# Token-major projections in pairs with 512 moving channels, and each convolution tap over all 512 tokens

## The chip, the cores and the metric

The kernel runs on one core of a Trainium2 chip. The metric is device time in microseconds (us). TensorE is called PE below, VectorE DVE, ScalarE ACT, GpSimd POOL, and the engine that issues the DMAs SP.

## What is computed

A decoder trunk of two layers on 512 tokens of 1024 channels, in float32:

```python
for l in range(L):
    h = rms_norm(x, attn_pre_g[l])
    u = jnp.einsum('bsd,de->bse', h, w_in[l])          # 1024 -> 10 blocks of 256
    u_conv, rq, rk, rv, rg, mq, mk, mv, u_pool = jnp.split(u, [...], axis=-1)
    y_a = conv_mixer(u_conv, ...)      # GLU, causal depthwise conv of 31 taps, LayerNorm, silu
    y_b = retention(rq, rk, rv, rg, ...)   # 4 heads, chunks of 128 tokens, group norm, gate
    y_c = moba_attention(mq, mk, mv)   # with 512 tokens in blocks of 256: causal attention
    y_d = pool_mixer(u_pool, ...)      # causal means over 2, 4, 8, 16 tokens
    y = jnp.einsum('bse,ed->bsd', jnp.concatenate([y_a, y_b, y_c, y_d], axis=-1), w_out[l])
    x = x + rms_norm(y, attn_post_g[l])
    h = rms_norm(x, ffn_pre_g[l])
    f = silu(h @ w_gate[l]) * (h @ w_up[l])            # 1024 -> 2816
    x = x + rms_norm(f @ w_down[l], ffn_post_g[l])
```

## The kernel before

**Numbers in two halves.** Each float32 matrix product is three float16 products (high x high, high x low, low x high; `split3`, L504). Weights come as slots of 128x2048 float32 (1 MB) in four parts. SP loads a part into one of four raw buffers (L443) once the buffer is free, that is once DVE has read it; ACT rounds it to a high half (`split_hi`, L790) and DVE takes the low half (`split_lo`, L1158). A split slot lies in a ring of eight; slot n may be written once PE has finished with slot n-8. The first three slots have raw homes of their own.

**PE's program** is a list of units (L89 to L97). W_in has ten slots of 256 channels. They go in three groups (MQ, MK, CONV_A, CONV_G; then MV, RQ, RK, RV; then POOL, RG), each group first for tokens 0 to 255 (s=0), then for 256 to 511 (s=1). A unit is 48 matmuls: two of something, eight k-tiles, three products. Slots in TOKEN_MAJOR hold 128 tokens still and move the slot's 256 channels (shown as ps<-ring,hT); the others hold 128 channels still and move 256 tokens (ps<-hT,ring). After the ten slots come W_out (OUT units, 512 wide, ps<-ring,U), gate and up, and down.

**Small work between.** Between any two triples of matmuls (a tick, `TICK0`, L109) PE may run small products: transposes, attention (moba) and retention products. The table AT (L120) says at which tick each stands. PE takes its instructions strictly in this order, so a small product whose input is late holds everything behind it. `moba_stage` 0 to 5 is attention for s=0, 6 to 11 for s=1; bank 5 of PSUM is shared by moba_Y, conv_T, conv_Y, ret_O and ret_Y, one after the other (`take`, L497).

**DVE and ACT** run lists written by hand (L1533, L1000). The convolution (`conv`, L1270) works on channels by tokens: for s=0 and for s=1 each, 31 taps x 2 channel blocks = 62 operations of 128x256 (two L1284, the rest L1287), each multiplying shifted input by a per-partition weight and adding to `cacc`. It can begin for s=0 once glu(0) has written its input, and s=1 once glu(1) has. Its 62 operations are strewn between others: splits, `m_max` (L1469, the row maxima of attention), rotations (L1334 to L1339), norms, `pool_windows` (L1438 to L1456). `conv_T` on PE transposes the finished `cacc`, `conv_norm` (L1300) takes its statistics.

## Time and profile before

| what | value |
|---|---|
| three runs | 1099.81, 1101.53 and 2939.43 us, median 1101.53 |
| the profiled execution: its own time | 1100.66 us |
| its span in the trace | 1098.9 us, 16669 instructions |
| PE matmul busy | 98% of the span, 6662 matmuls |
| DVE busy | 57%, 1419 instructions |
| ACT busy | 37%, 810 instructions |
| W_in stage of layer 0, first unit to first OUT unit | 14.17 to 164.77 us |
| W_in stage of layer 1 (its first transposes ahead of the first unit included) | 555.57 to 701.97 us |

The page adds up each engine's busy time over the whole span. What a change in the W_in stage is worth is read from the timeline of that stage: which engine's row says that it sat idle, and on whom. The mean duration of one matmul is longer than the distance from one to the next, because they overlap; the distance is a row's length divided by its count, after the last one's tail (0.16 us at 256 columns, 0.27 us at 512) is taken off. For DVE a lone operation's duration is about 0.08 us longer than the distance between two back to back.

### The profile page before, as it was taken

Reading aid. Unit: us, or ns where it says so; the run is one execution under the profiler, and the core shown is the slowest. Engines: PE = TensorE matmul, PEld = TensorE weight load, DVE = VectorE, ACT = ScalarE, POOL = GpSimd, SP = SyncE. Lnnn points to the kernel's source line nnn. Section 1 sums busy time; section 2 is a strip of 40 time slices with the busy share of each in tenths; the row PEclk is TensorE's granted clock in tenths of the full one; section 3 lists DMA queues with packets and bytes.
Section 4 is the critical chain, followed back from the end, with each engine's and each line's share of the span. In section 5 each row is a group of like instructions: output and inputs, shape, how many; then the busy total and the mean of one; then the engine's idle time right before and its main releaser. Section 6 shows DMA issues by size and latency. Waiting matters only on the chain.

```text
span 1098.9 us, 16669 instructions
## 1 busy us (share of the span) xinstructions
PE 1081.2 (98%) x6662; PEld 656.5 (60%) x6662; DVE 621.1 (57%) x1419; ACT 410.0 (37%) x810; POOL 5.2 (0%) x18
## 2 busy tenths in 40 slices
PE   8999999999999999999999999999999999999997
PEld 5887894695444444444488888748744444444443
DVE  6998998973432433322579889898633433422014
ACT  5636355553332332221244464456532322331000
POOL 1000000000000000000000000000000000000000
PEclk9999999999999999999999999999999999999999
DMA  8513212254324323323023150134623323232001
GB/s 310 172 56 102 92 40 97 96 166 142 115 77 153 109 83 115 114 79 115 1 79 115 40 151 5 43 111 154 183 86 115 116 96 115 91 101 77 1 20 58
DMA packets 58173, 109.64 MB, mean 100 GB/s; under 512 B 7025, under 2 KB 7281, under 8 KB 57969
## 3 DMA queue, kind: packets, MB, share of 16 engines
q1 hardware_dynamic: 58096, 108.58, 30.8%
q8 instruction: 53, 0.87, 0.3%
q14 instruction: 24, 0.19, 0.1%
HBM read 106.46 MB, written 2.10 MB: 99 GB/s over the span
## 4 chain that ended last, share of the span: by engine, by line
PE 91%; DMA 3%; DVE 3%; ACT 1%; SPq 1%; issue 1%; ACTq 0%; DVEq 0%
PE ps L508 84%; DMA raw<-weights_dram 3%; PE ps L512 3%; PE ps L716 1%; PE ps L700 1%; DVE ring L1158 1%; DMA xs<-x_dram 1%; DVE E L1287 1%; ACT ring L786 0%; PE ps L635 0%; SPq L453 0%; ACT gbc L786 0%; PE ps L677 0%; PE ps L638 0%; PE ps L620 0%
## 5 line engine op out<-in xcount | busy, mean ns | idle before, releaser
L508 PE MATMUL ps<-hT,ring 128*128 128x512 f16 (+1 forms) x3264 | 547.4, 329 | 0.0
L508 PEld LDWEIGHTS ps<-hT,ring 128*128 128x128 f16 x3264 | 319.1, 98 | 221.4
L508 PE MATMUL ps<-ring,U 128*128 128x512 f16 x1440 | 313.4, 379 | 0.0
L1158 DVE SCALAR_TENSOR_TENSOR ring<-raw,ring 128x512 f16<-128x512 f32 x368 | 231.2, 685 | 89.4 <-ACT ring L786 88.7
L786 ACT ACTIVATE ring<-raw 128x512 f16<-128x512 f32 x368 | 208.1, 621 | 126.6 <-PE ps L508 80.4
L508 PEld LDWEIGHTS ps<-ring,U 128*128 128x128 f16 x1440 | 140.8, 98 | 167.2 <-issue 0.3
L1490 DVE SCALAR_TENSOR_TENSOR R<-ps,R 128x512 f32<-128x512 f32 (+1 forms) x52 | 31.7, 609 | 256.2 <-ACT R L961 255.9
L508 PE MATMUL ps<-ring,hT 128*128 128x256 f16 x1152 | 133.3, 273 | 1.4 <-DVE hT L1247 1.3
L961 ACT ACTIVATE R<-ps 128x512 f32<-128x512 f32 (+1 forms) x52 | 27.6, 530 | 276.1 <-PE ps L508 276.0
L508 PEld LDWEIGHTS ps<-ring,hT 128*128 128x128 f16 x1152 | 112.1, 98 | 16.1 <-issue 1.9
L1287 DVE SCALAR_TENSOR_TENSOR E<-E,par 128x256 f32<-128x256 f32 x240 | 102.1, 479 | 0.2
L1175 DVE TENSOR_SCALAR small<-small 128x1 f32<-128x1 f32 x31 | 4.7, 150 | 84.9 <-ACT sink L796 76.3
L796 ACT ACTIVATE sink<-ps 128x1024 bf16<-128x1024 f32 x15 | 15.2, 1017 | 90.6 <-PE ps L508 90.6
L1497 DVE TENSOR_TENSOR U<-R,U 128x512 f16<-128x512 f32 (+1 forms) x52 | 31.2, 600 | 0.0
L786 ACT ACTIVATE gbc<-ps 128x128 f32<-128x128 f32 (+3 forms) x32 | 13.9, 434 | 42.6 <-PE ps L716 34.0
L786 ACT ACTIVATE U<-R 128x512 f16<-128x512 f32 (+1 forms) x52 | 28.9, 556 | 2.1 <-DVE R L1490 2.1
L786 ACT ACTIVATE U<-ps 128x256 f32<-128x256 f32 (+2 forms) x48 | 22.0, 485 | 17.9 <-PE ps L508 8.8
L512 PE MATMUL ps<-cst,E 128*128 128x128 f32 x176 | 24.0, 274 | 3.2 <-DVE E L1239 2.8
L807 ACT ACTIVATE ps<-xs 128x1024 f32<-128x1024 f32 x16 | 16.3, 1022 | 26.6 <-DVE xs L1207 21.3
L935 ACT ACTIVATE gbc<-ps,small 128x128 f32<-128x128 f32 (+3 forms) x32 | 16.8, 526 | 23.0 <-DVE small L1469 22.6
L512 PEld LDWEIGHTS ps<-cst,E 128*128 128x128 f32 x176 | 20.1, 141 | 6.7 <-DVE E L1239 2.7
L786 ACT ACTIVATE hT<-ps 128x1024 f16<-128x1024 f32 x16 | 16.3, 1019 | 17.8 <-PE ps L512 17.8
(109 smaller groups left out, 498.9 us busy)
## 6 DMA issues: line engine op xcount, KB each, us to landing
raw<-weights_dram SPq DMA_DIRECT2D x368, 256.0 KB, 3.3
gbc<-gains_dram SPq DMA_DIRECT2D x8, 512.0 KB, 6.2
xs<-x_dram SPq DMA_DIRECT2D x4, 512.0 KB, 7.0
U<-weights_dram SPq DMA_DIRECT2D x8, 256.0 KB, 7.9
out_dram<-xs SPq DMA_DIRECT2D x8, 256.0 KB, 2.0
cst<-consts_dram SPq DMA_DIRECT2D x1, 1296.0 KB, 12.2
bd<-pool_w_dram SPq DMA_DIRECT2D x8, 16.0 KB, 9.8
par<-params_dram SPq DMA_DIRECT2D x1, 76.0 KB, 6.7
```

Of the source, the lines that this page charges most:

```text
L508: ins = mm(dst, st, mv_, start=first and i == 0, stop=last and i == 2, **kw)
L512: return nc.tensor.transpose(dst, src, ident)
L700: mm(bank[b][:, 0:P * (t + 1)], mqT[r, t % 2, h // 2, :], mkT[r, h // 2, 0:P * (t + 1)], start=False, stop=True, skip_group_check=True).th ...
L786: return A(dst, src, ACT.Copy, scale=scale)
L796: A(sink[:, :], pair(t), ACT.Square, scale=UNSCALE * DM ** -0.5, accum_out=ssq[:, t:t + 1]).then_inc(y_sq, 1)
L807: A(pair(t), xs[:, t, :], ACT.Square, scale=DM ** -0.5, accum_out=ssq[:, 4 + t:5 + t]).then_inc(x_sq, 1)
L935: A(pr[:, h % 2, 0:w], bank[(4, 6)[h % 2]][:, 0:w], ACT.Exp, bias=nms[:, c:c + 1], accum_out=sums[:, c:c + 1]).then_inc(mP, 1)
L961: A(sil[:, n % 2, 0:P * len(tiles)], gu_tiles(f, tiles)[0], ACT.Silu, scale=UNSCALE).then_inc(sil_done, 1)
L1158: V.scalar_tensor_tensor(out=ring[:, slot % RING, 1, raw_part(part)], in0=raw_home(n)[0], scalar=W_SCALE, in1=ring[:, slot % RING, 0, raw_ ...
L1287: ins = V.scalar_tensor_tensor(out=cacc[:, c, :], in0=src, scalar=w, in1=cacc[:, c, :], op0=ALU.mult, op1=ALU.add)
L1490: V.scalar_tensor_tensor(out=fbuf[:, n % 2, 0:w], in0=gu_tiles(f, tiles)[1], scalar=UNSCALE * A_SCALE, in1=sil[:, n % 2, 0:w], op0=ALU.mul ...
L1497: V.tensor_tensor(fT[:, 1, f, span(tiles)], fbuf[:, n % 2, 0:w], fT[:, 0, f, span(tiles)], ALU.subtract).then_inc(f_lo, 1)
```

## The change

1. The token-major slots become pairs: MQ with MK, MV with RV, RQ with RK. The weights of a pair are laid out so that its eight parts are the eight k-tiles, each with 512 channels (256 of either). A unit is now one tile of 128 tokens against 512 moving channels: 24 matmuls instead of 2 x 24 with 256. In the first unit of each pair PE waits for each part by itself (all eight of both slots within that unit). Pairs finish tile by tile, so ACT copies (`moba_in`, `v_in`) and DVE rotates (`ret_rotate`, `moba_rotate`) one tile of both members at a time: as many operations, of the same sizes.
2. The convolution's taps run over all 512 tokens: 62 operations of 128x512 in a layer in place of 124 of 128x256. They can begin only when glu(1) is done, and conv_T(0) can begin only when all are done.
3. `cn` moves into `cacc`; the scaling of queries by 1/8 moves from one ACT copy to another.
4. The tables AT and the lists of DVE and ACT are written anew around this; the groups are now MQ+MK, CONV_A, CONV_G; MV+RV, RQ+RK; POOL, RG. A token-major unit is 8 ticks of 512-column triples, the others 16 ticks of 256.

```diff
-MQ, MK, CONV_A, CONV_G, MV, RQ, RK, RV, POOL, RG = range(10)
+MQ, MK, CONV_A, CONV_G, MV, RV, RQ, RK, POOL, RG = range(10)
-TOKEN_MAJOR = (RQ, RK, RV, MQ, MK, MV)
+PAIRS = {MQ: MK, MV: RV, RQ: RK}
...
-    UNITS += [(c, HALVES[s]) for s in range(2) for c in group]
+    for tiles in HALVES:
+        for c in group:
+            if c in PAIRS:
+                UNITS += [(c, (t,)) for t in tiles]
+            elif c not in PAIRS.values():
+                UNITS.append((c, tiles))
...
-        ("moba_stage", 6): 184, ("conv_T", 0): 186, ("moba_stage", 7): 208, ("ret_T", 0): 211,
+        ("moba_stage", 6): 170, ("conv_T", 0): 172, ("moba_stage", 7): 183, ("ret_T", 0): 185,
...
+                if slot in PAIRS:
+                    if pre:
+                        pe.wait_ge(h_lo, xno(pre, l, t) + 1)
+                    take(i % 4, *pair_read(l, slot, t))
+                    for k in range(KT):
+                        if k:
+                            between(k)
+                        if FIRST_OF[slot] == i:
+                            pe.wait_ge(lo_split, PARTS * (l * SLOTS + slot) + k + 1)
+                        r, cols = (l * SLOTS + slot + k // PARTS) % RING, raw_part(k % PARTS)
+                        last = split3(bank[i % 4][:, :], [ring[:, r, 0, cols], ring[:, r, 1, cols]],
+                                      [hT[:, 0, k, tok(t)], hT[:, 1, k, tok(t)]], k == 0, k == KT - 1, False)
...
             def conv_T(l, s):
-                pe.wait_ge(conv_sb, hs(l, s))
+                pe.wait_ge(conv_sb, l + 1)
                 take(5, convN_sb, 2 * hs(l, s))
...
-            def conv(l, s, n):
+            def conv(l, n):
+                if l not in taps_done:
+                    taps_done[l] = 0
+                    dve.wait_ge(hb_sb, hs(l, 1))
...
-                    src = hbuf[:, c, HALF * s + k:HALF * s + k + HALF]
+                    src = hbuf[:, c, k:k + S]
...
+                moba_rotate(l, 3)
+                glu(l, 1)
+                split_lo(z + 9)
+                conv(l, 7)
                 m_max(l, 0, 0)
-                conv(l, 0, 1)
                 m_max(l, 0, 1)
...
-                conv_norm(l, 0, lambda: conv(l, 1, 1))
-                ret_rotate(l, 0, 1)
-                conv(l, 1, 1)
+                conv_norm(l, 0)
+                split_lo(z + 11)
                 m_max(l, 2, 2)
                 m_max(l, 2, 3)
-                conv(l, 1, 1)
-                split_lo(z + 10)
-                zero(l)
+                pool_windows(l, 0)
                 ret_mask(l, 0)
```

**The first unit.** On PE, at the first matmuls of layer 0's W_in stage (unit MQ, then MK), before:

```order
L508 MATMUL ps<-ring,hT 128x256 [waits lo_split,h_lo]
L508 MATMUL ps<-ring,hT 128x256 x5
L508 MATMUL ps<-ring,hT 128x256 [waits lo_split]
L508 MATMUL ps<-ring,hT 128x256 x5
L508 MATMUL ps<-ring,hT 128x256 [waits lo_split]
L508 MATMUL ps<-ring,hT 128x256 x5
L508 MATMUL ps<-ring,hT 128x256 [waits lo_split]
L508 MATMUL ps<-ring,hT 128x256 x5
L508 MATMUL ps<-ring,hT 128x256 [waits h_lo]
L508 MATMUL ps<-ring,hT 128x256 x23
```

The same engine after the change, from the fourth k-tile of the first tile on:

```order
L520 MATMUL ps<-ring,hT 128x512 [waits lo_split]
L520 MATMUL ps<-ring,hT 128x512 x2
L520 MATMUL ps<-ring,hT 128x512 [waits lo_split]
L520 MATMUL ps<-ring,hT 128x512 x2
L520 MATMUL ps<-ring,hT 128x512 [waits lo_split]
L520 MATMUL ps<-ring,hT 128x512 x2
L520 MATMUL ps<-ring,hT 128x512 [waits lo_split]
L520 MATMUL ps<-ring,hT 128x512 x2
L520 MATMUL ps<-ring,hT 128x512 [waits lo_split]
L520 MATMUL ps<-ring,hT 128x512 x2
L520 MATMUL ps<-ring,hT 128x512 [waits h_lo]
L520 MATMUL ps<-ring,hT 128x512 x23
```

Before, four parts (one slot) are waited for in the first tile, one per two k-tiles, and the second slot comes a tile later; now all eight parts are waited for in the first tile, one per k-tile.

**Where the taps begin.** On DVE in layer 0, before, from glu(0) (E<-U,ps) to the first taps (E<-E,par) and the split of slot 7 (ring<-raw):

```order
L1263 SCALAR_TENSOR_TENSOR E<-U,ps 128x2x256 [waits glu_th,unit_done]
L1284 TENSOR_SCALAR E<-E,par 128x256 [waits hT_ps,hb_sb]
L1284 TENSOR_SCALAR E<-E,par 128x256
L1287 SCALAR_TENSOR_TENSOR E<-E,par 128x256 [waits dve_tick] x8
L1158 SCALAR_TENSOR_TENSOR ring<-raw,ring 128x512 [waits hi_split] x4
L1287 SCALAR_TENSOR_TENSOR E<-E,par 128x256 [waits dve_tick] x18
```

After, from the end of the last moba rotation over glu(1) to the taps and the first row maxima:

```order
L1355 TENSOR_TENSOR U<-E 128x8x16 [waits dve_tick]
L1279 SCALAR_TENSOR_TENSOR E<-U,ps 128x2x256 [waits glu_th,unit_done]
L1174 SCALAR_TENSOR_TENSOR ring<-raw,ring 128x512 [waits hi_split] x4
L1300 TENSOR_SCALAR E<-E,par 128x512 [waits hT_ps,hb_sb]
L1300 TENSOR_SCALAR E<-E,par 128x512
L1303 SCALAR_TENSOR_TENSOR E<-E,par 128x512 [waits dve_tick] x5
L1477 TENSOR_REDUCE small<-ps 128x1 [waits mS_ps] x2
L1303 SCALAR_TENSOR_TENSOR E<-E,par 128x512 [waits dve_tick] x12
L1477 TENSOR_REDUCE small<-ps 128x1 [waits mS_ps] x2
L1303 SCALAR_TENSOR_TENSOR E<-E,par 128x512 [waits dve_tick] x9
```

The taps moved from behind glu(0) to behind glu(1) and the split of slot 9, and m_max(0,0) stands behind seven wide taps.

**Where the taps end.** On DVE in layer 0, before, from the row scaling of attention tile 1 over the split of slot 9 to the end of half 0's taps and the low half of moba's output (U<-ps,U):

```order
L1480 TENSOR_TENSOR E<-ps,small 128x256 [waits dve_tick]
L1158 SCALAR_TENSOR_TENSOR ring<-raw,ring 128x512 [waits hi_split] x4
L1287 SCALAR_TENSOR_TENSOR E<-E,par 128x256 [waits dve_tick] x2
L1254 SCALAR_TENSOR_TENSOR U<-ps,U 128x2x256 [waits moba_hi]
L1469 TENSOR_REDUCE small<-ps 128x1 [waits mP,mS_ps] x2
L1303 BN_STATS small<-ps 128x6 [waits convT_ps]
```

After, the same place:

```order
L1303 SCALAR_TENSOR_TENSOR E<-E,par 128x512 [waits dve_tick] x2
L1174 SCALAR_TENSOR_TENSOR ring<-raw,ring 128x512 [waits hi_split] x4
L1303 SCALAR_TENSOR_TENSOR E<-E,par 128x512 [waits dve_tick] x12
L1270 SCALAR_TENSOR_TENSOR U<-ps,U 128x2x256 [waits moba_hi]
L1477 TENSOR_REDUCE small<-ps 128x1 [waits mP,mS_ps] x2
L1319 BN_STATS small<-ps 128x6 [waits convT_ps]
```

The last two narrow taps of a half have become the last twelve wide taps, ahead of the low half of moba_Y(0) that frees bank 5, and of conv_norm.

**Who waits.** On PE in layer 0, before, from the S products of attention stage 6 over conv_T(0) (ps<-cst,E):

```order
L700 MATMUL ps<-U 128x384 x2
L508 MATMUL ps<-ring,hT 128x256 x6
L512 MATMUL ps<-cst,E 128x128 [waits moba_y,conv_sb]
L512 MATMUL ps<-cst,E 128x128 x3
L508 MATMUL ps<-ring,hT 128x256 x18
L508 MATMUL ps<-ring,hT 128x256 [waits mv_sb]
```

After, the same place:

```order
L717 MATMUL ps<-U 128x384 x2
L520 MATMUL ps<-hT,ring 128x256 x6
L524 MATMUL ps<-cst,E 128x128 [waits moba_y,conv_sb]
L524 MATMUL ps<-cst,E 128x128 x3
L520 MATMUL ps<-hT,ring 128x256 x12
L520 MATMUL ps<-hT,ring 128x256 [waits v_sb,lo_split]
```

Both times conv_T(0) stands six matmuls behind stage 6 and waits for the low half of moba_Y(0) and for conv_sb; before, conv_sb meant the 62 narrow taps of half 0 with 18 and more matmuls of RQ behind it, now it means all 62 wide taps, and the stream behind it is that of POOL (ps<-hT,ring).

## Rows read from the trace of the kernel before

**Rows 1.** The page: busy time of each engine; its row of the granted clock.

```profile
PE 1081.2 (98%) x6662; PEld 656.5 (60%) x6662; DVE 621.1 (57%) x1419; ACT 410.0 (37%) x810; POOL 5.2 (0%) x18
...
PEclk9999999999999999999999999999999999999999
```

**Rows 2.** Busy time in two stretches: start:end length, each engine's busy us (instructions), clock, DMA.

```profile
14.17:164.77 150.60, 146.92 (x1293) 127.32 (x1294) 136.33 (x346) 77.26 (x166) 2.57 (x8) 1.00 0.35 111
...
555.57:701.97 146.40, 145.12 (x1293) 127.59 (x1292) 128.28 (x334) 70.86 (x154) 0.00 (x0) 1.00 0.26 80
```

**Rows 3.** Timeline of PE: start, length (us), line, operation, count [idle before <-releaser].

```profile
14.17 10.93 PE L508 MATMUL ps<-ring,hT 128*128 128x256 f16 x96 [0.69 <-DVE hT L1247]
...
59.40 0.27 PE L697 MATMUL ps<-cst 128*128 128x128 bf16 x2 [0.34 <-ACT U L786]
...
61.34 2.13 PE L508 MATMUL ps<-ring,hT 128*128 128x256 f16 x18
...
118.50 9.01 PE L508 MATMUL ps<-ring,hT 128*128 128x256 f16 x81
...
164.77 4.70 PE L508 MATMUL ps<-ring,U 128*128 128x512 f16 x21
...
169.74 10.52 PE L508 MATMUL ps<-ring,U 128*128 128x512 f16 x48
...
555.57 1.04 PE L512 MATMUL ps<-cst,E 128*128 128x128 f32 x8
...
602.08 5.40 PE L508 MATMUL ps<-ring,hT 128*128 128x256 f16 x48
...
701.97 5.34 PE L508 MATMUL ps<-ring,U 128*128 128x512 f16 x24
```

**Rows 4.** Timeline of DVE at the start of layer 0.

```profile
13.99 1.89 DVE L1158 SCALAR_TENSOR_TENSOR ring<-raw,ring 128x512 f16<-128x512 f32 x3
15.79 1.22 DVE L1247 SCALAR_TENSOR_TENSOR hT<-ps,hT 128x1024 f16<-128x1024 f32 x1
16.92 4.90 DVE L1158 SCALAR_TENSOR_TENSOR ring<-U,ring 128x512 f16<-128x512 f32 x8
```

**Rows 5.** Timeline of ACT: the first halves of two slots' splits.

```profile
42.50 1.24 ACT L786 ACTIVATE ring<-raw 128x512 f16<-128x512 f32 x2 [0.58 <-DMA raw<-weights_dram]
...
47.15 1.36 ACT L786 ACTIVATE ring<-raw 128x512 f16<-128x512 f32 x2 [0.63 <-DMA raw<-weights_dram]
```

**Rows 6.** Timeline of DVE, layer 0: taps, rotation, windows, split, norms.

```profile
53.62 7.21 DVE L1287 SCALAR_TENSOR_TENSOR E<-E,par 128x256 f32<-128x256 f32 x18
...
89.93 1.02 DVE L1469 TENSOR_REDUCE small<-ps 128x1 f32<-128x384 f32 x2
...
111.35 1.29 DVE L1469 TENSOR_REDUCE small<-ps 128x1 f32<-128x512 f32 x2 [0.26 <-PE ps L700]
...
120.37 0.68 DVE L1334 TENSOR_TENSOR E<-ps,cst 128x512 f32<-128x512 f32 x1
...
122.36 0.59 DVE L1390 TENSOR_TENSOR U<-U,ps 64x128 f32<-64x128 f32 x2
...
137.30 0.72 DVE L1438 TENSOR_TENSOR Z<-U 128x540 f32<-128x540 f32 x1
...
142.35 3.65 DVE L1287 SCALAR_TENSOR_TENSOR E<-E,par 128x256 f32<-128x256 f32 x9
...
154.11 2.49 DVE L1158 SCALAR_TENSOR_TENSOR ring<-raw,ring 128x512 f16<-128x512 f32 x4
...
163.33 0.76 DVE L1303 BATCH_NORM_STATS2 small<-ps 128x6 f32<-128x256 f32 x2 [0.20 <-PE ps L512]
...
166.95 1.11 DVE L1400 BATCH_NORM_STATS2 small<-U 128x6 f32<-128x64 f32 x8
...
170.86 0.17 DVE L1412 SCALAR_TENSOR_TENSOR small<-small 128x8 f32<-128x8 f32 x1
```

**Rows 7.** Groups by shape: line, engine, op, shapes, count | busy us, mean ns.

```profile
L1220 DVE SCALAR_TENSOR_TENSOR ps<-ps,small,gbc 128x512 f32<-128x512 f32 x8 | 6.0, 755 | 0.1
```

More of the change, by code:

```diff
@@ L98 @@
 NU = len(UNITS)
-UNIT_AT = {(slot, t): i for i, (slot, tiles) in enumerate(UNITS) for t in tiles}
+UNIT_AT = {(c, t): i for i, (slot, tiles) in enumerate(UNITS) for c in {slot, PAIRS.get(slot, slot)} for t in tiles}
 FIRST_OF = {slot: min(UNIT_AT[slot, t] for t in TILES) for slot in range(SLOTS)}
@@ L127 @@
-        ("ret_S", 1): 225, ("ret_O", 1): 229, ("moba_stage", 9): 258, ("ret_T", 2): 277,
-        ("moba_stage", 10): 280, ("ret_S", 2): 280, ("moba_stage", 11): 285, ("moba_Y", 1): 293,
-        ("ret_Y", 0): 299, ("ret_T", 3): 302, ("pool_Y", 0): 304, ("ret_O", 2): 304, ("ret_S", 3): 307,
-        ("ret_O", 3): 310, ("conv_T", 1): 315, ("conv_Y", 1): 327, ("ret_Y", 1): 343, ("pool_Y", 1): 350,
-        ("fpre_T", 0): 372, ("fpre_T", 1): 374, ("fpre_T", 2): 415, ("fpre_T", 3): 438, ("pre_T", 0): 955,
@@ new lines @@
+        ("moba_stage", 1): 114, ("moba_T", 2): 122, ("moba_stage", 2): 126, ("moba_stage", 3): 131,
+        ("moba_stage", 4): 142, ("moba_stage", 5): 148, ("moba_T", 3): 160, ("moba_Y", 0): 165,
+        ("moba_stage", 6): 170, ("conv_T", 0): 172, ("moba_stage", 7): 183, ("ret_T", 0): 185,
+        ("conv_Y", 0): 187, ("ret_S", 0): 190, ("ret_O", 0): 192, ("ret_T", 1): 192, ("moba_stage", 8): 192,
+        ("ret_S", 1): 196, ("ret_O", 1): 199, ("moba_stage", 9): 202, ("ret_T", 2): 206,
+        ("moba_stage", 10): 206, ("moba_stage", 11): 206, ("pool_Y", 0): 206, ("moba_Y", 1): 208,
@@ L145 @@
     },
 ]
+E_COLS = 7 * 2 * HALF + 2 * (CW - 1 + S) + 4
 PAR = {}
@@ L394, in unit_bank, with tile_bank, of_tile @@
             return UNIT_AT[(slot, 2 * s)] % 4
+        def tile_bank(slot, t):
+            return bank[UNIT_AT[(slot, t)] % 4][:, :]
+        def of_tile(buf, t):
+            return buf[:, 2 * G * t:2 * G * (t + 1)]
         def gu_tiles(f, tiles):
@@ L528, in unit @@
                 between(0)
-                by_parts = l == 0 and i == 0
-                if FIRST_OF[slot] == i and not by_parts:
+                if FIRST_OF[slot] == i and slot not in PAIRS:
                     pe.wait_ge(lo_split, PARTS * (l * SLOTS + slot + 1))
@@ L544, in unit @@
                                 between(KT * c + k)
[L545 to L552 removed]
+                            cols, rows = slice(P * c, P * (c + 1)), half(s)
                             last = split3(b256(b)[:, c, :], [w[0][:, k, cols], w[1][:, k, cols]],
[L554 to L555 removed]
+                                          [hT[:, 0, k, rows], hT[:, 1, k, rows]], k == 0, k == KT - 1, True)
                 elif wide:
@@ L663, in conv_T @@
                     for c in range(2):
-                        last = transpose(b256(5)[:, t, P * c:P * (c + 1)], cacc[:, c, tok(t)])
+                        last = transpose(b256(5)[:, t, P * c:P * (c + 1)], cacc[:, c, tok(2 * s + t)])
                 last.then_inc(convT_ps, 1)
@@ L1726 @@
         weights[:, slot] = by_col[:, :, :, blk].transpose(0, 2, 1, 3).reshape(L, P, SLOT)
+    for slot, other in PAIRS.items():
+        both = by_col[:, :, :, [BLOCK_OF[slot], BLOCK_OF[other]]].reshape(L, 2, KT // 2, P, 2 * G)
+        weights[:, slot:slot + 2] = both.transpose(0, 1, 3, 2, 4).reshape(L, 2, P, SLOT)
     out_k = [k + c for k in (4, 0, 2, 6) for c in range(2)]
```

347 lines of the change are left out of this document (153 added, 194 removed).

## The prediction, made before the changed kernel was run

> **What bounds the kernel now.** I read the page first: PE is busy for 98% of the span at the full granted clock, 2.4 GHz, DVE for 57% [rows 1]. So nothing is won by relieving DVE or ACT unless PE waits for them, and PE idles 17.7 us in all (1098.9 less 1081.2), part of it at the start and the end, which the change leaves alone. The change lies in the W_in stages, so I cut the busy times by these: in layer 0 PE is busy 146.9 of 150.6 us, DVE 136.3; in layer 1 145.1 of 146.4 and 128.3 [rows 2]. There both engines are nearly full, and PE's own waits, which the timeline marks (an example is the 0.34 us ahead of the first attention product), come to only 3.7 and 1.3 us [rows 2, 3]. The third view is the timeline of PE: where the units begin and how far apart matmuls start. The fourth is that of DVE: what its blocks cost, since the change makes PE wait for all of the convolution at once.
>
> **PE's stream.** 96 matmuls of 256 columns in 10.93 us look slow, but there the first weights are still arriving. Away from it 81 take 9.01 us: less the tail, 0.1093 us each. 48 of 512 columns take 10.52, less the tail 0.2135 each [rows 3]. Two narrow ones cost 0.2186, one wide one 0.2135: 0.0051 us saved on each of 576 pairs, **2.9 us**, 1.45 a layer. All the columns are still moved; halving the count of matmuls saves next to nothing. What such a small gain rests on is the distance between starts, not the mean duration.
>
> Of this the Trainium skill, TensorE: Matmul & The Clock Gate, section "Back-to-back issue gap", says that in a sustained stream 512 columns take about 131 ns per matmul. By it the pairs would save 576 x (0.2186 - 0.131), 50 us. The 48 wide matmuls of these rows started 0.2135 us apart, so I follow the rows and leave this as a rival.
>
> **The first unit.** Before, tile 0 needs four parts; slot 1 comes a tile later. Now tile 0 needs eight. DVE's three parts from 13.99 are ready at 14.7, 15.3 and 15.9; then stands h_lo of tile 1 (1.22 us), and the parts of slot 1 come from 16.92 on at 0.60 us each, the first at 17.60 [rows 4]. PE starts at 14.17 and spends 3 x 0.2135 = 0.64 us per k-tile, so it wants part 4 at 16.75 and gets it 0.85 to 0.9 us later. After that DVE delivers every 0.60, faster than PE eats. Cost **0.9 us**, once: in layer 1 these slots were split long before. Nothing gives it back, since PE is the bound.
>
> **The taps.** 18 narrow ones take 7.21 us, less 0.08 for the last 0.396 each [rows 6]. A wide one with a per-partition scalar isn't in the trace as a tap. The nearest row is L1220, the same operation with such a scalar on 128x512: 0.755 us alone [rows 7], less 0.08 of overlap 0.67. Lower bound: the split, 512 wide without such a scalar, 2.49 us for four, 0.60 each [rows 6]; upper bound 0.755. I take 0.67: 62 cost 41.5 us. The 124 narrow ones at 0.396 cost 49 back to back, and about 3 more where they are strewn singly. DVE gains some 10 us a layer. That alone is worth nothing to PE, beyond the 3.7 and 1.3 us of waits.
>
> The Trainium skill, VectorE: DVE Perf Modes, section on the TRN2 errata, gives 58 cycles plus the elements at 0.96 GHz for an operation out of SBUF, 0.33 and 0.59 us. By it DVE would gain only 124 x 0.33 - 62 x 0.59 = 4 us a layer, but with wide taps of 0.59 the chain below would end 5 us earlier and PE's floor would hold. The narrow taps' 0.396 us shows that a tap costs more than that formula has, so I keep the rows' price.
>
> **When the taps can begin.** Here is the price of the change. They wait for glu(1), which was behind the second unit of CONV_G. In layer 0 PE reached the MV unit at 61.34 [rows 3]. Subtract attention stage 0, which now comes later (0.6), the waits up to there (about 0.9) and the stream (0.5), add the first unit's 0.9: 60.2. Then come on ACT the tanh (0.6) and four high halves of slot 9 (2.2), on DVE the last low half (0.7): taps from **63.7**. Until then DVE has only splits. Each slot takes about 4.65 us round the four raw buffers (42.50 to 47.15 [rows 5]), so slots 5 to 9 from 41 on end at about 64 too; this doesn't come first, but it would not let the taps begin earlier. In layer 1 MV began at 602.08 [rows 3]; less stages 0 and 1 and one transpose (2.0) and 0.5: 599.6, taps from 603.1.
>
> **The chain of DVE.** From there to the end of the taps: 41.5, eight short row maxima 2.2, two rotations of 2.0 (120.37 to 122.36), two scalings 1.1, the split of slot 10, 2.4, and the low half of moba_Y, 0.6 [rows 6]. Sum 51.8: 115.5 in layer 0. PE wants conv_T(0) 64 ticks of 0.641, 12 of 0.328 and about 10 us of small products after 60.2: 115.1. So this wait is 0.4 us at my tap price, and 5 us more at the upper one (60 x 0.085). Behind conv_T(0) stand attention stage 7, ret_T(0) and everything up to W_out.
>
> Then DVE still has, up to ret_mask(3), four splits 9.6; four pairs of row maxima (1.02 and 1.29 a pair, two of each, less the overlap) 4.4; conv_norm 3.6 (163.33 to 166.95); pool_windows 5.0 (137.30 to 142.35); ret_norm 4.1 (166.95 to 170.86 and its length); two rotations 4.0; masks, states, products, scalings and low halves about 9.6 [rows 6]. Sum 40.3. Without a wait that is 155.8. But now PE's small products stand close (stages 7 to 11, all ret products in 40 ticks of 0.328 us), so DVE waits for PE and PE for DVE in turn, where formerly single taps filled such holes. I count 5 us of such idle time, as between 2 and 9: a dozen hand-overs at 0.2 to 0.8 us, sized like the waits in [rows 3]. So ret_mask(3) at 160.8, ret_O(3) and conv_T(1) 1.6: W_out begins at 162.4, against 164.77: **-2.4 us**. Layer 1: 603.1 + 51.8 + 40.3 + 5 + 1.6 = 701.8, against 701.97: **-0.2 us**. PE's own floor would be 159.1 and 700.5 (busy 145.1 less 1.45, and 0.9 in layer 0), so the DVE chain ends last in both layers, by 1 to 3 us.
>
> **W_out.** DVE has about 26 us of work from its begin to the low half of ret_y(1), and PE needs that 40 ticks of 0.641 and 2 us later, 28. I take no wait; it would be 1 or 2 us a layer if the chain comes late. Copies and rotations are as many and as wide as before and lie beside PE. The feed-forward stages are untouched: 0.
>
> **Sum.** 1098.9 - 2.4 - 0.2 = 1096.3 us of span. The profiled execution took 1100.66, 1.8 more than its span, and the median of the runs is 0.9 above that: 1096.3 + 1.8 + 0.9 = **1099 us**. In this sum stream and first unit are already inside the layers' ends.
>
> **Rivals.**
> - *All waits go (0.15).* If the hand-overs cost no more than 2 us, PE's floor holds: -5.7 in layer 0, -1.5 in layer 1, 1094. For it: DVE's total falls to about 126 and 118 us in stages of 146. Against it: the work is pressed into the last 95 us.
> - *The convolution becomes the bound (0.27, of it 0.02 beyond 2%).* Wide taps near 0.75 and hand-overs of 9 us: 5 + 4 more in each layer, and 2 in W_out, about +15 in the worst case, +6 (1107) in its middle. It decides from a tap of 0.70 on, where conv_T(0) waits over 2 us and DVE ends later than before.
> - *The matmuls get cheap (0.01).* 50 us less, 1050. Against it stand the distances in [rows 3].
> - *The first unit waits much longer (0.02).* If slot 1's parts were late by a whole landing (some 3 to 5 us), 1103. Against it: both slots come early in [rows 4].
>
> **How the numbers follow.** My forecast, DVE's and PE's ends within a few us of each other, has 0.55: 1096 to 1103. The likeliest is its sum, 1099. Range: down to the floor, less a little, 1092; up into the slower rival, 1110. Over 2% is 22 us, about what a measurement of this kernel can tell from no change: a gain of that size exceeds all of PE's idle time, so 0.015; a loss of that size needs 10 us in each layer, 0.025; within 2%, 0.96.
>
> **What would show it.** 576 matmuls ps<-ring,hT of 512 columns at 0.2135 us; a wait of 0.9 us in the first unit; 120 taps of 128x512, mean 0.75 us, 0.67 apart; DVE's busy time down by 18 to 21 us to about 601; conv_T(0) waiting 0 to 3 us for DVE; new short waits of PE between conv_T(0) and W_out, 3 to 6 us a layer; W_out beginning near 162 and near 699. Wrong would be: taps starting well after 64, a W_in stage longer than 150 us, or a wait in W_out.

## The result: 6.5 us slower, where 2 us less were forecast

The changed kernel took 1107.66 us (median of 4 runs, 1106.72 to 1109.29) against 1101.12 for the kernel before in the same comparison, a ratio of 1.0062 with a 95% interval from 1.0050 to 1.0074. (One execution of the kernel before took 2939.43 us; it is in that median of four, but the ratio goes by the fast runs alone.) By the 2% bound that is no change, and inside the range. But the forecast had the sign wrong. The profiled execution took 1107.27 us with a span of 1105.4, against 1098.9 before.

The page of the changed kernel, to be read beside [rows 1]: busy times and the two groups that are new.

```profile
span 1105.4 us, 15389 instructions
...
PE 1080.5 (98%) x6086; PEld 600.5 (54%) x6086; DVE 607.5 (55%) x1295; ACT 408.2 (37%) x810; POOL 5.1 (0%) x18
...
L520 PE MATMUL ps<-ring,hT 128*128 128x512 f16 x576 | 128.3, 379 | 1.4 <-DVE ring L1174 0.7
...
L1303 DVE SCALAR_TENSOR_TENSOR E<-E,par 128x512 f32<-128x512 f32 x120 | 81.1, 744 | 0.0
```

Every engine has less to do, and the span is longer. The W_in stages answer to [rows 2]: start:end, length, then busy us (instructions) of PE, PEld, DVE, ACT and POOL, granted clock, DMA share, GB/s.

```profile
13.69:165.07 151.38, 145.78 (x1004) 99.56 (x1005) 130.77 (x282) 75.89 (x167) 2.57 (x8) 1.00 0.35 113
555.85:707.27 151.42, 145.52 (x1005) 99.68 (x1004) 125.39 (x276) 71.67 (x158) 0.00 (x0) 1.00 0.25 79
```

Layer 0's stage is 0.8 us longer than before, layer 1's 5.0. From W_out of layer 0 (165.07) to layer 1's W_in (555.85) it is 390.8 us in both kernels. From W_out of layer 1 to the end it is 1.2 us more. The first unit begins 0.5 us earlier; I count that to the start-up and not to the change, since in the traces of the variants below, all with the same start, it begins anywhere from 13.34 to 14.24 us. Sum: 0.8 + 5.0 + 1.2 - 0.5 = 6.5.

The place shows when the last 50 us ahead of W_out are set beside each other, layer 0 and layer 1 (same columns). Before:

```profile
114.77:164.77 50.00, 49.76 (x445) 44.39 (x445) 46.56 (x134) 20.58 (x43) 0.00 (x0) 1.00 0.20 64
651.97:701.97 50.00, 49.83 (x449) 44.48 (x446) 46.52 (x136) 20.64 (x43) 0.00 (x0) 1.00 0.20 59
```

And after, from conv_T(0) on (115.07 and 657.07):

```profile
115.07:165.07 50.00, 46.02 (x388) 38.66 (x387) 41.74 (x116) 32.49 (x74) 0.00 (x0) 1.00 0.28 91
657.07:707.27 50.20, 45.93 (x388) 38.61 (x387) 41.76 (x116) 33.88 (x76) 0.00 (x0) 1.00 0.28 90
```

PE idled 0.2 us there and now idles 4.0 and 4.3; DVE idled 3.4 and now idles 8.3 and 8.4. Both engines wait for each other more, with less work on either. The timeline of PE names the two waits (start, length, operation, count, [idle before <- releaser]); layer 0, then layer 1:

```profile
115.07 0.60 PE L524 MATMUL ps<-cst,E 128*128 128x128 f32 x4
115.51 3.77 PE L520 MATMUL ps<-hT,ring 128*128 128x256 f16 x33
120.61 0.52 PE L524 MATMUL ps<-cst,gbc 128*128 128x128 f32 x3 [1.34 <-ACT E L865]
...
128.91 1.10 PE L652 MATMUL ps<-U,R 128*128 128x64 f32 x8 [1.27 <-DVE R L1387]
...
662.61 0.52 PE L524 MATMUL ps<-cst,gbc 128*128 128x128 f32 x3 [1.67 <-ACT E L865]
...
670.90 1.10 PE L652 MATMUL ps<-U,R 128*128 128x64 f32 x8 [1.76 <-DVE R L1387]
```

The first row is conv_T(0). 33 narrow matmuls (11 ticks, 3.8 us; in layer 1 it is 10 ticks) later stage 7 wants bank 5, which conv_T(0) filled and which comes free only after conv_norm(0) on DVE and conv_scale(0) on ACT (L865). Next ret_O(0) waits for ret_mask(0) (L1387). On DVE the rows between are, in this order (the last of each block):

```profile
115.71 0.76 DVE L1319 BATCH_NORM_STATS2 small<-ps 128x6 f32<-128x256 f32 x2 [0.18 <-PE ps L524]
...
119.25 0.16 DVE L1331 SCALAR_TENSOR_TENSOR small<-small 128x2 f32<-128x2 f32 x1
119.33 2.49 DVE L1174 SCALAR_TENSOR_TENSOR ring<-raw,ring 128x512 f16<-128x512 f32 x4
122.12 1.02 DVE L1477 TENSOR_REDUCE small<-ps 128x1 f32<-128x384 f32 x2 [0.30 <-PE ps L717]
123.06 0.71 DVE L1446 TENSOR_TENSOR Z<-U 128x540 f32<-128x540 f32 x1
...
127.64 0.42 DVE L1464 SCALAR_TENSOR_TENSOR Z<-E,U 64x256 f32<-64x256 f32 x1
128.10 0.76 DVE L1387 TENSOR_TENSOR R<-ps,cst 128x256 f32<-128x256 f32 x2
```

conv_norm(0) 3.7 us, a split 2.5, two maxima 1.0, pool_windows(0) 5.0, then the mask: 13 us of DVE, of which 12.6 busy, while PE has only 10.9 us of work between conv_T(0) and ret_O(0) (10.4 in layer 1). Before, conv_T(0) ran at 90.49 us and 66 narrow matmuls stood between it and the next product:

```profile
90.49 0.60 PE L512 MATMUL ps<-cst,E 128*128 128x128 f32 x4
90.93 7.37 PE L508 MATMUL ps<-ring,hT 128*128 128x256 f16 x66
98.14 0.49 PE L512 MATMUL ps<-cst,gbc 128*128 128x128 f32 x3
```

### The profile page after: what moved, and what is told of

Its sections match the earlier page's. It is cut to its first block, busy times and chain, and to the rows that moved or that the text cites. A ratio compares the mean times of both kernels' runs of the same rounds, so it can differ in the third digit from the quotient of the medians.

```text
span 1105.4 us, 15389 instructions
## 1 busy us (share of the span) xinstructions
PE 1080.5 (98%) x6086; PEld 600.5 (54%) x6086; DVE 607.5 (55%) x1295; ACT 408.2 (37%) x810; POOL 5.1 (0%) x18
## 4 chain that ended last, share of the span: by engine, by line
PE 93%; DVE 4%; DMA 1%; ACT 1%; issue 1%; SPq 0%; ACTq 0%; DVEq 0%
PE ps L520 85%; PE ps L524 3%; PE ps L733 1%; PE ps L717 1%; PE ps L652 1%; DMA xs<-x_dram 1%; DVE ring L1174 0%; DMA raw<-weights_dram 0%; DVE E L1303 0%; PE ps L637 0%; PE ps L694 0%; ACT E L865 0%; DVE Z L1464 0%; ACT gbc L803 0%; DVE small L1155 0%
## 5 line engine op out<-in xcount | busy, mean ns | idle before, releaser
L803 ACT ACTIVATE ring<-raw 128x512 f16<-128x512 f32 x368 | 207.1, 621 | 123.6 <-PE ps L520 78.7
L520 PE MATMUL ps<-ring,hT 128*128 128x512 f16 x576 | 128.3, 379 | 1.4 <-DVE ring L1174 0.7
L520 PEld LDWEIGHTS ps<-ring,hT 128*128 128x128 f16 x576 | 56.2, 98 | 65.2 <-DVE ring L1174 2.3
L1303 DVE SCALAR_TENSOR_TENSOR E<-E,par 128x512 f32<-128x512 f32 x120 | 81.1, 744 | 0.0
L803 ACT ACTIVATE U<-ps 128x256 f32<-128x256 f32 (+2 forms) x48 | 22.1, 488 | 51.2 <-PE ps L524 32.5
L803 ACT ACTIVATE U<-R 128x512 f16<-128x512 f32 (+1 forms) x52 | 28.9, 556 | 3.2 <-DVE R L1498 3.2
L803 ACT ACTIVATE hT<-ps 128x1024 f16<-128x1024 f32 x16 | 16.2, 1017 | 28.3 <-PE ps L524 28.3
L803 ACT ACTIVATE gbc<-ps 128x128 f32<-128x128 f32 (+3 forms) x32 | 13.9, 435 | 27.0 <-PE ps L733 15.4
```

The costliest lines, as they stand in the source:

```text
L520: ins = mm(dst, st, mv_, start=first and i == 0, stop=last and i == 2, **kw)
L803: return A(dst, src, ACT.Copy, scale=scale)
L1303: ins = V.scalar_tensor_tensor(out=cacc[:, c, :], in0=src, scalar=w, in1=cacc[:, c, :], op0=ALU.mult, op1=ALU.add)
```

## Experiments: what the loss hangs on

All ratios are against the kernel before, which ran beside each on the same chip; the changed kernel stands at 1.0062.

**Too much work ahead of conv_T(0)?** The forecast's slower rival was that the taps become the bound.

```diff
-                for i in range(taps_done[l], min(taps_done[l] + n, 2 * CW)):
+                for i in range(taps_done[l], min(taps_done[l] + n, 2 * CW - 20)):
```

> The changed kernel with the last 20 of the 62 wide taps of each layer left out (the convolution is then incomplete), 13.3 us less work for DVE ahead of conv_T(0). Theory VOLUME (too much work on DVE ahead of conv_T(0), or a tap price that makes the convolution the bound): the waits of PE behind conv_T(0) go and the time falls to 1.000 of before or under. Theory CHAIN or PLACE (latency behind conv_T(0)): DVE just waits longer for conv_T(0), stage 7 waits 1.3 and 1.7 us and ret_O(0) 1.3 and 1.8 us as they do now, time 1.005 to 1.006 of before.

1107.48 us, 1.0060 (1.0048 to 1.0072). DVE is busy 38.72 of the 52.25 us from the first tap to conv_T(0), 13 us less than in the changed kernel, and nothing changes: stage 7 waits 1.34 and 1.67, ret_O(0) 1.27 and 1.76, to the hundredth. At 0.66 us a tap, neither the volume ahead of conv_T(0) nor the price of a tap costs anything.

```profile
62.82:115.07 52.25, 51.38 (x289) 28.34 (x288) 38.72 (x70) 14.00 (x41) 0.00 (x0) 1.00 0.12 39
```

The other direction, each wide tap as two of 256 at its place:

```diff
-                        ins = V.scalar_tensor_tensor(out=cacc[:, c, :], in0=src, scalar=w,
+                        for s in range(2):
+                            ins = V.scalar_tensor_tensor(out=cacc[:, c, half(s)], in0=src[:, half(s)], scalar=w,
```

> The changed kernel with each wide tap as two of 256 tokens at the same place, still behind glu(1): 62 x (2 x 0.396 - 0.662) = 8.1 us more for DVE ahead of conv_T(0) in each layer. Price of the row: PE waits some 8 us more for conv_T(0) in each layer, so 16 us and, if TensorE's clock falls behind so long a wait, up to 4 us more in each layer: 1.020 to 1.029 of before. If DVE had room ahead of conv_T(0): under 1.012.

1123.68, 1.0197 (1.0179 to 1.0216), just under the 1.020 that the price of the row gave. PE waits at conv_T(0) itself, now 3.35 and 2.70 us, and further up for ACT's steps of attention (1.45 and 1.10 us in layer 0, 1.53, 1.28 and 1.10 in layer 1), and part of the work behind the waits runs at a lower clock (last section). So the wide taps had just made room; without them the joined convolution would have cost some 16 us more.

**Products merely too early?**

```diff
-        ("moba_stage", 6): 170, ("conv_T", 0): 172, ("moba_stage", 7): 183, ("ret_T", 0): 185,
-        ("conv_Y", 0): 187, ("ret_S", 0): 190,
+        ("moba_stage", 6): 170, ("conv_T", 0): 172, ("moba_stage", 7): 187, ("ret_T", 0): 188,
+        ("conv_Y", 0): 189, ("ret_S", 0): 190,
```

> The changed kernel with attention stage 7, ret_T(0) and conv_Y(0) moved to later ticks (187 to 189), in both layers, so that matmuls of W_in fill the 1.34 and 1.67 us that stage 7 waits. ret_O(0) stays at tick 192, since the unit at tick 192 needs the rotation behind it. Nothing is left out. Theory PLACE (the products merely stand too early): stage 7 waits for nothing, the waits of the layer fall by 1.3 and 1.7 us, time 1.006 - 0.0027, near 1.0035 of before. Theory CHAIN (DVE's work between conv_T(0) and ret_mask(0), some 13 us, is longer than PE's 11): the wait only moves, stage 7 is free of it, ret_O(0) waits 2.6 and 3.4 us instead of 1.27 and 1.76, and the time stays at 1.006 of before.

1108.91, 1.0075 (1.0063 to 1.0087). Stage 7's wait is gone, and ret_O(0) waits 2.07 us in both layers, ret_T(0) 0.64. The wait moved, as theory CHAIN has it: with ret_T(0)'s it is 2.7 us in each layer, for 2.9 and 3.4. The medians differ by 1.3 us and their intervals overlap; in the trace the groups behind the longer wait of layer 0 run at a lower clock, which costs 1.3 us (last section).

```profile
123.33 0.63 PE L524 MATMUL ps<-cst,R 128*128 128x128 f32 x4 [0.64 <-ACT gbc L951]
128.70 1.64 PE L652 MATMUL ps<-U,R 128*128 128x64 f32 x8 [2.07 <-DVE R L1387]
```

**Cutting the chain.** One Newton step instead of three in conv_norm(0), or pool_windows(0) reduced to one memset, or both.

```diff
-                n = tick(rsqrt(slice(8, 10), fill))
+                n = tick(rsqrt(slice(8, 10), fill, 3 if s else 1))
...
+                if s == 0:
+                    V.memset(pooled_w, 0.0).then_inc(pool_sb, 1)
+                    return
```

> The changed kernel with one instead of three Newton steps in conv_norm(0) in both layers (the convolution's scale of the first half is then less exact), 1.38 us less of DVE between conv_T(0) and stage 7. Theory CHAIN: all behind stage 7 comes 1.3 us earlier in each layer, stage 7 waits 0 and 0.3 us, ret_O(0) still 1.3 and 1.8 us, time 2.7 us lower, 1.0035 of before. If it is the products' distance behind (PLACE) or ACT that decides: the wait comes back within the layer, over 1.005.

1104.81, 1.0031 (1.0017 to 1.0044). Stage 7 waits 0 and 0.29, ret_O(0) 1.26 and 1.76 as before.

> The changed kernel with pool_windows(0) cut down to one memset in both layers (the pooling branch of the first half is left out), 4.7 us less of DVE ahead of ret_mask(0). Theory CHAIN: ret_O(0) waits under 0.5 us instead of 1.27 and 1.76, stage 7 as now, time 2 to 3.5 us lower, 1.003 to 1.0045 of before, with no more than that, since the rest of DVE's work waits for PE's products. Theory VOLUME behind conv_T(0): DVE's 4.7 us are worth 4.7 us in each layer, 0.998 of before.

1104.83, 1.0032 (1.0021 to 1.0043). Stage 7 waits 1.33 and 1.67 as ever, ret_O(0) nothing and 0.38. 4.7 us of DVE work left out were worth 1.5 us a layer: what the wait had.

> The changed kernel with both cuts at once, one Newton step instead of three in conv_norm(0) (less exact) and pool_windows(0) reduced to a memset (the pooling branch of the first half left out), in both layers. Alone each brought 2.9 us. Theory CHAIN (conv_norm(0) and pool_windows(0) stand one after the other in one chain from conv_T(0) to ret_mask(0)): both gains add, stage 7 and ret_O(0) wait under 0.7 us together per layer, 5.8 us under the changed kernel, 1.0005 of before, so that these two waits account for about the whole loss. If the two cuts relieve the same wait, or another wait takes over: 1.002 to 1.003.

1101.65, 1.0003 (0.9994 to 1.0012). Both gains add: 6.0 of the 6.5 us, and what is left is within the interval. So the two waits are as large as the loss. They are not each layer's own loss: in the traces layer 0's W_in stage is now 1.3 us shorter than before the change, while from one W_out to the next, layer 1's W_in stage included, it takes 539.4 us against 537.2 before and 542.2 in the changed kernel. Layer 1 keeps other waits (below).

**Moving instead of cutting.** The first try put the mask ahead of all of pool_windows(0):

```diff
-                pool_windows(l, 0)
                 ret_mask(l, 0)
+                pool_windows(l, 0)
```

> The changed kernel with ret_mask(0) ahead of pool_windows(0) on DVE, in both layers; nothing is left out. Theory CHAIN: ret_O(0) waits at most 0.8 us instead of 1.27 and 1.76; DVE stands idle some 3.5 us until ret_S(0) is there, and works this off in its idle stretches behind; time 1.0035 to 1.005 of before. Theory VOLUME (DVE is the bound from there to W_out): the idle 3.5 us come back as waits before W_out, 1.008 of before or more. Theory PLACE has no say on it beyond CHAIN's.

1118.00, 1.0154 (1.0141 to 1.0167). The time lies where theory VOLUME put it (1.008 or more), but neither theory had the mechanism. ret_O(0) indeed stopped waiting for the mask, but ret_state(0) (L1398) now stood behind pool_windows(0), and it frees bank 6 for stage 8 (L714). I had read who waits for the step moved forward, not who waits for the one behind it.

```profile
127.65 0.71 DVE L1446 TENSOR_TENSOR Z<-U 128x540 f32<-128x540 f32 x1
...
133.29 0.60 DVE L1398 TENSOR_TENSOR U<-U,ps 64x128 f32<-64x128 f32 x2
```

```profile
133.94 0.23 PE L714 MATMUL ps<-cst 128*128 128x128 bf16 x1 [3.12 <-DVE U L1398]
134.10 1.60 PE L717 MATMUL ps<-U 64*128 64x512 f32 x4
```

Dividing it helps: the sums stay ahead of the mask, and the last four operations (1.75 us) fill the 1.1 us in which DVE waited for ret_O(0).

```diff
+            def pool_means(l, s):
+                for i, (r, c, v) in enumerate(sums_):
+                    ins = V.scalar_tensor_tensor(out=pooled[r, c, :], in0=v, scalar=1.0 / WINDOWS[i],
...
                 ret_mask(l, 0)
+                pool_means(l, 0)
                 conv_out(l, 0)
```

> The changed kernel with pool_windows(0) divided: the window sums stay ahead of ret_mask(0), its last four operations (1.75 us) go behind it, where DVE waited 1.1 us for ret_O(0); stage 7 at 185/186, ret_T(0) at 187/188, conv_Y(0) one later, stage 4 of layer 1 at 143, conv_Y(1) at 234. Nothing is left out. Theory CHAIN: stage 7 and ret_O(0) together wait 1.1 us a layer less (the last third of pool_windows comes off the path to ret_mask(0)), 1.0015 to 1.004 of before. Theory VOLUME: 1.005 or more.

1104.63, 1.0034 (1.0021 to 1.0046), the best complete version of the changed kernel, 3 us under it and still 3.6 over the kernel before. ret_O(0) waits 0.17 and 0.38, stage 7 0.68 and 0.38. Not all of the 3 us belong to the division: the ticks moved with it, and in layer 1 a wait of attention ahead of conv_T(0) fell from 0.93 to 0.18 us.

Putting pool_windows(0) at the end of the stage did worse:

```diff
-                pool_windows(l, 0)
                 ret_mask(l, 0)
...
                 lo_of(b256(5), moba_hi, 4, l, 1, A_SCALE, moba_y)
-                split_lo(z + 14)
+                pool_windows(l, 0)
                 ret_out(l, 0)
```

> The changed kernel with pool_windows(0) (5.0 us of DVE) taken out from between conv_T(0) and ret_mask(0) and put behind the last rotation, near the end of the W_in stage, where the splits of slots 13 to 15 are moved back for it; pool_Y(0) goes to tick 227, stage 7 to 185/186, ret_T(0) to 188, conv_Y(0) to 189, conv_Y(1) to 236. Nothing is left out. Theory CHAIN (13 us of DVE between conv_T(0) and ret_mask(0) against 11 us of PE): stage 7 and ret_O(0) together wait under 1 us instead of 2.6 and 3.4, the time falls by 4 to 5 us to 1.002 of before. Theory VOLUME (DVE is full from conv_T(0) to W_out, so 5 us put elsewhere come back as a wait before or in W_out): 1.006 or more.

1169.86, 1.0628 (1.0610 to 1.0647). The two waits fell to 0.69 and 0.38 as forecast, but I had moved DVE's splits and not ACT's. ACT stood 8.21 us in the high half of a slot whose raw buffers DVE had not read, with attention's copies queued behind it, and PE waited 10.23, 5.42 and 8.99 us in layer 0. The mean granted clock of the execution fell to 0.971, from 0.998; of its 1167.8 us that accounts for 31 us at most (an estimate from these figures). That the time is beyond theory VOLUME's 1.006 says nothing for it.

```profile
153.04 1.15 ACT L803 ACTIVATE ring<-raw 128x512 f16<-128x512 f32 x2 [8.21 <-DMA raw<-weights_dram]
```

The same with ACT's high halves moved back too:

```diff
-                split_hi(z + 14)
                 ret_T_copy(l, 2)
...
+                split_hi(z + 14)
                 from_unit(l, POOL, 1, ubuf[:, :, 16 + HALF:16 + S], pool_u)
```

> The changed kernel with pool_windows(0) near the end of the W_in stage, as in the run before, now with ACT's high halves of slots 14 to 16 moved back as well, since in that run ACT stood in the high half of slot 14, whose raw buffers wait for DVE's low half of slot 13. Nothing is left out. Theory CHAIN: stage 7, ret_T(0) and ret_O(0) wait about 1.1 us together in each layer (instead of 2.9 and 3.4), no other wait grows by more than 1 us; 1.002 to 1.004 of before. Theory VOLUME: the 5 us of pool_windows(0) come back as waits at pool_Y(0) or in W_out, 1.006 or more.

1115.26, 1.0127 (1.0110 to 1.0144). With ACT's moved too, the two waits are 0.68 and 0.38 in layer 0 and 0.38 each in layer 1, and others take their place: 1.30 and 0.88 (moba_Y(1) for m_norm), 1.25 and 1.03 (ret_S(3)), and 2.39 in W_out of both, for a bank that gate(1) frees late. In layer 0 the 24 matmuls behind that last wait take 7.03 us where 24 such take 5.34. Theory VOLUME has the range and the wait in W_out: undivided, the 5 us did not fit behind the mask, and not at this place either. Other places were not tried.

**The pairs without the joined convolution.** Taps of 256 tokens again, the first half's from glu(0) on, conv_T(0) at tick 132 or 134 instead of 172, in three placements.

```diff
-                    src = hbuf[:, c, k:k + S]
+                    src = hbuf[:, c, HALF * s + k:HALF * s + k + HALF]
+                    acc = cacc[:, c, half(s)]
...
-        ("moba_stage", 6): 170, ("conv_T", 0): 172, ("moba_stage", 7): 183, ("ret_T", 0): 185,
-        ("conv_Y", 0): 187, ("ret_S", 0): 190,
+        ("moba_stage", 6): 170, ("conv_T", 0): 132, ("moba_stage", 7): 183, ("ret_T", 0): 186,
+        ("conv_Y", 0): 151, ("ret_S", 0): 190,
```

> The pairs without the other part of the change: taps of 256 tokens, those of the first half from glu(0) on, conv_T(0) at tick 132, conv_norm(0) and conv_scale(0) under attention stages 3 and 4, conv_Y(0) at 151; the last taps of the second half stand where DVE waited for PE. Nothing is left out. DVE has 8 us a layer more to do than in the changed kernel. Theory CHAIN (joining the halves is what costs, since it puts conv_norm(0) into the densest stretch): stage 7 and ret_O(0) wait under 0.5 us, W_out begins near 162 and near 699 us, and the time is 0.994 to 0.998 of before. Theory VOLUME: DVE's 16 us more come back as waits, 1.010 or more. Theory PAIRS (pairs of token-major slots are what costs): 1.004 to 1.006.

1115.30, 1.0129 (1.0113 to 1.0144). Stage 7 waits for nothing, since conv_norm(0) is gone from there. But taps ahead of glu(1) delayed it by 3.7 us, moba_T(2) waited 1.96 in layer 0, ret_O(0) 2.04 and 2.20. The time is in theory VOLUME's range. The second placement moves taps away from there:

```diff
                 split_lo(z + 5)
                 moba_rotate(l, 1)
-                conv(l, 5)
                 split_lo(z + 6)
-                conv(l, 5)
+                conv(l, 4)
                 split_lo(z + 7)
```

> Pairs with taps of 256 tokens as in the run with half taps, placed anew: 12 taps instead of 20 ahead of glu(1) (which came 3.7 us late), conv_T(0) at tick 134, stage 7 at 180 (DVE had waited 2.2 us for it), ret_T(0) at 185, conv_Y(1) at 233, conv_scale(1) ahead of the high half of slot 16, six taps less ahead of pool_windows(0). Nothing is left out. Theory CHAIN (what costs is work of DVE between products that stand close): the wait of 1.96 us ahead of moba_T(2) and most of the 2.0 and 2.2 us at ret_O(0) go, with them the stretch at half clock; 5 us a layer, 1.003 to 1.006 of before. Theory VOLUME (8 us a layer of narrow taps can't be placed): 1.010 or more.

1107.14, 1.0057 (1.0042 to 1.0072). moba_T(2) still waits 0.73, ret_O(0) 1.22 and 1.55, ret_S(3) 0.86 and 0.84. The time is the one that theory CHAIN forecast here (1.003 to 1.006), but also that of theory PAIRS in the run before. The third divides pool_windows(0) as above and moves taps from those places:

```diff
-                conv(l, 20)
+                conv(l, 17)
                 m_max(l, 0, 2)
...
                 ret_mask(l, 0)
+                pool_means(l, 0)
```

> The pairs with taps of 256 tokens (all of DVE's 13.6 us back), as in the tuned run, with pool_windows(0) divided around ret_mask(0), some taps moved from ahead of moba_T(2) and ret_state(2) to where DVE idled, and the splits of slots 15 and 16 behind conv_norm(1) and rg_tanh(1). Nothing is left out. If only the chain to ret_mask(0) and those places matter: the waits of 1.22 and 1.55 at ret_O(0), 0.73 at moba_T(2), 0.86 and 0.84 at ret_S(3) go, 4 to 5 us under the tuned run, 1.0015 to 1.003 of before. If DVE with narrow taps is full from conv_T(0) to W_out (it idled 2.8 us of 50 there), the waits come back elsewhere: 1.004 to 1.006.

1107.41, 1.0054 (1.0040 to 1.0067). ret_O(0) is down to 0.17 and 0.15, and in exchange 0.67 at stage 8, 0.34 at ret_O(1), 1.75 and 1.76 in W_out: the waits move along as fast as they are mended. The time fits "DVE is full", but DVE still idles 5.1 of the 50 us ahead of W_out (114.07 to 164.07), against 3.4 in the kernel before, so that DVE's volume binds these placements is not shown. Two things stay open. The wait at ret_O(0) stood in the first two placements too (2.04 and 2.20, 1.22 and 1.55), where the halves were not joined, so the joining alone does not account for it, only for stage 7's. And both tuned placements lie at 1.0054 and 1.0057, where theory PAIRS put them; no run has the joined convolution without the pairs, and whether the pairs alone could gain with a better order than mine, three tries don't settle.

**The width of the matmuls by itself.**

```diff
-                        last = split3(bank[i % 4][:, :], [ring[:, r, 0, cols], ring[:, r, 1, cols]],
+                        g = slice(G * m, G * (m + 1))
+                        last = split3(bank[i % 4][:, g], [ring[:, r, 0, cols][:, g], ring[:, r, 1, cols][:, g]],
```

> The changed kernel with each 512-wide matmul of a pair replaced by two of 256 columns, first half of the columns over all k-tiles, then the second; ticks and small products as in the changed kernel. 576 x 0.0051 = 2.9 us more of stream, and the first unit wants its parts twice as fast, which costs up to 2.4 us more there. If PE's stream sets the time wherever it does not wait: 3 to 5 us over the changed kernel, 1.009 to 1.011 of before. If DVE's chain sets the end of each W_in stage, the stream's part behind conv_T(0) (a third) is lost in the waits: 1.008 to 1.009. If wide matmuls save nothing at all: 1.006 to 1.008.

1112.82, 1.0104 (1.0091 to 1.0117), 5.2 us over the changed kernel's median, 4.2 between the traces. Of these 2.2 lie in the first unit, which waits 1.23 us instead of 0.74 and then for further parts. 1.3 us is a stretch of lower clock behind ret_O(0) in layer 1 (last section). What the width by itself is worth shows where both kernels run the same two tiles without a wait, with 48 wide matmuls (first row) and with 96 narrow ones:

```profile
37.19 10.52 PE L520 MATMUL ps<-ring,hT 128*128 128x512 f16 x48
39.38 10.64 PE L520 MATMUL ps<-ring,hT 128*128 128x256 f16 x96
```

That is 0.12 us on 48 pairs, 0.0025 each and 1.4 us in all, half of the 2.9 in the forecast. The group's busy time goes from 128.3 to 130.8 us, but 1.7 of these 2.5 lie in the first unit, where PE is held up for parts.

## Why the prediction failed, step by step

- **Stream: right in kind, half as large.** The forecast took 0.27 us off a row of wide matmuls as the last one's tail. By the rows themselves the tail is 0.16, as for narrow ones: 48 take 10.52 us and 24 take 5.34 [rows 3], so 24 more take 5.18, 0.2158 each and not 0.2135. The pairs save 0.0026 us each, 1.5 us in all and not 2.9; the run with narrow pairs gives 1.4. That is 0.7 us a layer, too little to turn the sign. The rival of cheap matmuls fell: 215.8 ns stand against the 131 that the Trainium skill has (TensorE: Matmul & The Clock Gate, "Back-to-back issue gap"). The formula in the same section for a matmul at full clock, N / 2.4 + 2.5, agrees with the rows at both widths: 109.2 for 109.2 ns, 215.8 for 215.8.
- **First unit: right.** 0.74 us for 0.9. The rival of a whole landing fell by this row, the rival that all waits go by the result.
- **Taps: right.** 0.662 us apart (12 in 8.03), mean 744 ns, begin at 62.82 and 604.06 for 63.7 and 603.1, conv_T(0) at 115.07 for 115.1 and without a wait. DVE's busy time fell by 13.6 us and not 18 to 21, though the taps' own group fell from 102.1 (L1287) to 81.1 us: many narrow ones had run in the pauses between the small operations of conv_norm and ret_norm, and those operations now show with their own time (read from the timelines, not tested). The rival "the convolution becomes the bound" gave 1107 for its middle, which is about the time measured. That is luck, since its mechanism fell: no wait at conv_T(0), and with a third of the taps left out nothing changes.
- **The rest of DVE's chain: its work right, its idle time wrong.** This is the step that failed: the term of 5 us for hand-overs, behind conv_T(0), in either layer. From the low half of moba_Y(0) to ret_mask(3) I had 40.3 us of work and "5 us of such idle time, as between 2 and 9". Measured, in layer 0 and layer 1 (columns as above: the third busy time is DVE's):

```profile
114.50:162.39 47.89, 44.48 (x375) 37.28 (x375) 39.91 (x115) 32.07 (x74) 0.00 (x0) 1.00 0.27 89
656.50:704.60 48.10, 44.07 (x374) 37.01 (x372) 39.95 (x115) 33.47 (x76) 0.00 (x0) 1.00 0.28 89
```

  39.91 and 39.95 us of work, 0.4 off; the idle time was 8.0 and 8.2. And from ret_mask(3) to W_out it took 2.7 us, not 1.6, as ret_O(3) and conv_T(1) take 2.0 us of PE by themselves and conv_T(1) waits for ACT's copy of ret_O(3) (0.57 us in layer 0, 0.24 in layer 1). With taps 1.0 us earlier than forecast, 162.4 - 1.0 + 2.6 + 1.1 = 165.1 in layer 0; with 1.0 later and their block 0.6 longer, 701.8 + 1.6 + 2.8 + 1.1 = 707.3 in layer 1. Those are the rows, 165.07 and 707.27.
- **How it came about.** I sized hand-overs "like the waits in [rows 3]", 0.2 to 0.8 us. Those were measured with single taps in every hole: DVE 46.56 of 50 us busy. Each of the two large ones had to be worked out by its own chain, and could have been. conv_norm starts 0.6 us behind conv_T(0) and takes 3.6, and ACT's two operations 1.0: 5.2 us, against conv_T(0)'s own 0.4 and 11 ticks of 0.328, 4.0. That is 1.2 us short, and with the 10 ticks of layer 1 1.5; measured were 1.34 and 1.67. And 12.8 us of DVE (conv_norm, split, maxima, windows, mask), which begin 0.2 us behind conv_T(0)'s end and have a hole of 0.3, stand against 20 ticks and the small products, 10.4: 2.9 us short. That is what PE waited in layer 0 up to ret_O(0), with 0.31 at ret_T(0). Nearly all of these durations lay in [rows 6], and I had added them into one sum per layer, as if only the sum mattered. The order of the two engines' work fixes who waits inside it.
- **Layer 1: a second slip.** My list of signs had "3 to 6 us" of new waits a layer, and that came true (4.0 and 4.3). The sum took them as offset by old waits, but [rows 2] has only 1.3 us of these in layer 1. A layer that had nothing to give back had to get slower by what was added: + 4.6 of idle, + 0.4 of PE's busy time (the stream's 0.7 should be there, but the last matmul ahead of each wait has its tail uncovered; this last is argued, not tested). Not all of the 4.6 are the two waits, which are 3.4: attention ahead of conv_T(0) waits 0.93 us for a copy on ACT that stands behind four high halves, where it waited 0.18 before. The floors that the forecast gave do not follow from its rows either: by [rows 2] and its own terms they are 164.77 - 3.7 - 1.45 + 0.9 = 160.5 and 701.97 - 1.3 - 1.45 = 699.2, not 159.1 and 700.5. It gave layer 0 too much to win and layer 1 too little; the sum is about the same.
- **W_out: wrong by 1.2 us, in layer 1.** PE waits 0.79 us there at conv_Y(1) for conv_scale(1) (L865). This is not conv_norm's latency again. DVE was through with conv_norm(1) at 711.18, the first row; ACT came to conv_scale(1) only at 712.91, because in its list the high halves of slot 16 of that layer (L803) stand ahead, and they waited for DMAs:

```profile
711.02 0.16 DVE L1331 SCALAR_TENSOR_TENSOR small<-small 128x2 f32<-128x2 f32 x1
...
710.10 0.63 ACT L803 ACTIVATE ring<-raw 128x512 f16<-128x512 f32 x1 [0.97 <-DMA raw<-weights_dram]
712.37 0.63 ACT L803 ACTIVATE ring<-raw 128x512 f16<-128x512 f32 x1 [1.64 <-DMA raw<-weights_dram]
712.91 1.00 ACT L865 ACTIVATE E<-ps,small 128x256 f32<-128x256 f32 x2
```

  In the kernel before, ACT began conv_scale(1) 0.04 us behind conv_norm(1) (at 703.63). How long the wait is depends on when those DMAs land: in the variants with this order of ACT it is between nothing and 0.97 us in layer 1. The runs that put conv_scale(1) ahead of those high halves (the second and third placement of the half taps, and pool_windows(0) late with ACT's high halves moved) do not have it. The other 0.4 us of W_out I did not trace. The forecast's own signs of being wrong had both come: a W_in stage longer than 150 us (151.4), and a wait in W_out.
